# Token sums on their own partitions: the five norms of a two-block transformer kernel

## The reference

```
def rms_norm(x, g):
    xf = x.astype(jnp.float32)
    y = xf * lax.rsqrt(jnp.mean(xf * xf, axis=-1, keepdims=True) + NORM_EPS)
    return (y * g.astype(jnp.float32)).astype(x.dtype)

def layer_norm(x, g, b):
    mu = jnp.mean(xf, axis=-1, keepdims=True)
    var = jnp.mean(jnp.square(xf - mu), axis=-1, keepdims=True)
    return ((xf - mu) * lax.rsqrt(var + LN_EPS) * g + b).astype(x.dtype)

first block:   h = rms_norm(x, g_mix); mem_kv = rms_norm(mem, g_mem) @ w_mem_kv; attention, convolution, gates
               x = x + merged @ w_o;  h = rms_norm(x, g_ffn);  x = x + ffn(h);  x = rms_norm(x, g_final)
second block:  x = layer_norm(ALPHA * x + y @ w_out);  x = layer_norm(ALPHA * x + relu(x @ w_up)^2 @ w_down)
```

## Time and profile before

| | |
|---|---|
| median of 3 runs | 2922.84 us (2919.59 to 2927.17) |
| profiled execution, its own time | 2926.96 us |
| span of that profile | 2925.2 us, mean granted clock 0.982 |
| PE, PEld busy | 2784.8 us (95%), 2242.1 us (77%) |
| DVE, ACT, POOL busy | 1921.9 us (66%), 1017.2 us (35%), 1459.6 us (50%) |

### The profile page before, as it was taken

One profiled execution on the slowest core, in us unless ns is written; L12 is line 12 of the kernel. 1 busy time (PEld: TensorE's weight loads), 2 busy tenths in 40 slices (PEclk: granted clock), 3 DMA queues, 4 the chain that ended last, 5 costly groups with the idle time before them and its releaser, 6 DMA issues.

```text
span 2925.2 us, 35308 instructions
## 1 busy us (share of the span) xinstructions
PE 2784.8 (95%) x12634; PEld 2242.1 (77%) x12634; DVE 1921.9 (66%) x2515; ACT 1017.2 (35%) x1882; POOL 1459.6 (50%) x960
## 2 busy tenths in 40 slices
PE   7989999999999999999999889999898999999997
PEld 4777878886776877777777678888676888888885
DVE  3888999998536656655657558888747533444437
ACT  3352301117413333333333456666514211222223
POOL 2433344441242566666765326666642656666662
PEclk9999999999999999999999999999899999999999
DMA  4211122221231112112112300010111121111112
GB/s 150 54 44 37 37 72 80 83 81 51 95 114 37 44 47 61 52 44 58 44 51 67 113 15 30 23 30 23 73 43 36 37 58 43 57 57 50 50 44 72
DMA packets 44474, 165.04 MB, mean 56 GB/s; under 512 B 4969, under 2 KB 5609, under 8 KB 43313
## 3 DMA queue, kind: packets, MB, share of 16 engines
q1 hardware_dynamic: 38464, 132.00, 14.5%
q10 hardware_dynamic: 5872, 31.23, 2.8%
HBM read 145.61 MB, written 16.78 MB: 56 GB/s over the span
## 4 chain that ended last, share of the span: by engine, by line
PE 68%; DVE 10%; issue 6%; POOL 6%; POOLq 4%; ACT 4%; DMA 1%; DVEq 1%; ACTq 0%; SPq 0%
PE dense L800 9%; PE dense L801 9%; PE dense L804 9%; POOL w_lo L670 4%; PE dense L1265 3%; PE dense L1266 3%; PE dense L1268 3%; PE dense L1307 2%; PE side L1244 2%; PE dense L1308 2%; PE dense L1309 2%; PE side L1246 2%; PE side L1245 2%; PE side L1439 2%; PE side L1440 2%
## 5 line engine op out<-in xcount | busy, mean ns | idle before, releaser
L586 POOL TENSOR_TENSOR w_hi<-raw,zero 128x1024 fp32r<-128x1024 f32 x101 | 206.4, 2044 | 660.5 <-PE dense L804 464.7
L670 POOL TENSOR_TENSOR w_lo<-raw,w_hi 128x512 fp32r<-128x512 f32 x230 | 334.5, 1457 | 305.6 <-ACT w_hi L1858 177.4
L800 PE MATMUL dense<-a_hi,w_hi 128*128 128x512 f32 x944 | 373.6, 396 | 10.2 <-POOL w_lo L588 3.2
L801 PE MATMUL dense<-a_lo,w_hi 128*128 128x512 f32 x944 | 370.0, 392 | 0.0
L804 PE MATMUL dense<-a_hi,w_lo 128*128 128x512 f32 x944 | 292.4, 391 | 0.0
L588 POOL TENSOR_TENSOR w_lo<-raw,w_hi 128x1024 fp32r<-128x1024 f32 x101 | 270.5, 2678 | 7.9
L800 PEld LDWEIGHTS dense<-a_hi,w_hi 128*128 128x128 f32 x944 | 178.6, 189 | 52.1 <-issue 6.2
L804 PEld LDWEIGHTS dense<-a_hi,w_lo 128*128 128x128 f32 x944 | 178.5, 189 | 37.8
L801 PEld LDWEIGHTS dense<-a_lo,w_hi 128*128 128x128 f32 x944 | 178.7, 189 | 35.6
L644 POOL TENSOR_TENSOR stick_weights<-stick_weights,stay 128x511 f32<-128x511 f32 (+2 forms) x144 | 133.9, 932 | 112.2 <-DVE stay L2844 112.2
L800 PE MATMUL dense<-b_hi,w_hi 128*128 128x512 f32 x480 | 187.6, 391 | 0.2
(11 more groups left out here) (384 smaller groups left out, 7338.4 us busy)
## 6 DMA issues: line engine op xcount, KB each, us to landing
raw<-in_w_stream SPq DMA_DIRECT2D x229, 512.0 KB, 3.6
x_in<-in_x_t SPq DMA_DIRECT2D x8, 512.0 KB, 7.4
spill_gate<-T ACTq DMA_DIRECT2D x8, 512.0 KB, 2.6
spill_part<-gates ACTq DMA_DIRECT2D x8, 512.0 KB, 2.6
back<-spill_gate ACTq DMA_DIRECT2D x8, 512.0 KB, 3.8
back<-spill_part ACTq DMA_DIRECT2D x8, 512.0 KB, 4.7
x_res<-in_x_t ACTq DMA_DIRECT2D x2, 2048.0 KB, 9.1
spill_x<-x_res ACTq DMA_DIRECT2D x1, 4096.0 KB, 14.4
```

Of the source, the lines that this page charges most:

```text
L586: pool.tensor_tensor(w_hi[:, r % 2, :], raw[:, r, :], zero[:, 0:1].broadcast_to([P, D]), ALU.add).then_inc(weights_rounded, 1)
L670: return pool.tensor_tensor(w_lo[:, s, half], src, w_hi[:, s, half].bitcast(F32), ALU.subtract)
L800: pe.matmul(o, w_hi[:, slot, w], hi[:, k, x], start=b == 0, stop=False)
L801: pe.matmul(o, w_hi[:, slot, w], lo[:, k, x], start=False, stop=False)
```

## The change

The square and residual terms become the stationary operand and one column of a constant matrix, now holding 1/1024, the moving one: `own_part` issues four one-column products for 512 tokens, and the mean of each token comes out on its own partition, in four columns of `side[:, 0]`. The DVE step `own_sums` goes; ACT's root reads the four PSUM columns itself in norms 0 to 2 and for the memory. Norms 3 and 4 get `own_variance`, four small DVE operations. The mean is still spread over all partitions by 512-column products (`mean_part`), and the means are summed a second time as one-column products. `diagonal` goes; `spread_columns` multiplies the identity by a column of inverse roots read as a 128x128 broadcast, four products of 128 columns. In norm 0, DVE adds the first half's squares in pairs, so that four terms are left in place of eight.

```diff
-MATRICES = {"ident": 104, "ones": 104.5, "causal_q": 107, "strict_q": 107.5}
+MATRICES = {"ident": 104, "mean": 104.5, "causal_q": 107, "strict_q": 107.5}
...
-            def sum_part(src, c, at, start, stop):
-
-                return pe.matmul(side[:, at, c], ones[:, :], src[:, c], start=start, stop=stop)
+            def mean_part(src, h, start, stop):
+
+                return pe.matmul(side[:, 1, cols(h)], mean[:, :], src[:, cols(h)], start=start, stop=stop)
+
+            def own_part(to, src, start, stop):
+
+                for n in range(to.shape[-1]):
+                    last = pe.matmul(to[:, n:n + 1], src[:, P * n:P * n + P], mean[:, 0:1], start=start and n == 0, stop=stop,
+                                     skip_group_check=True)
+                return last
+
+            def spread_columns(to, values):
+
+                for n in range(values.shape[-1]):
+                    last = pe.matmul(to[:, P * n:P * n + P], values[:, n:n + 1].broadcast_to([P, P]), ident[:, :], start=True,
+                                     stop=True, skip_group_check=True)
+                return last
...
             def first_sums(h):
-                for k in range(KB):
-                    pe.wait_ge(x_squared, KB * h + k + 1)
-                    src = x_squares[:, k, :] if h else T[:, k // 2, cols(k % 2)]
-                    last = pe.matmul(side[:, 0, cols(h)], ones[:, :], src, start=k == 0, stop=k == KB - 1)
+                terms = KB if h else KB // 2
+                for k in range(terms):
+                    pe.wait_ge(x_squared, KB * h + k + 1) if h else pe.wait_ge(x_paired, k + 1)
+                    last = own_part(own_squares(h), x_squares[:, k, :] if h else T[:, k, cols(0)], k == 0, k == terms - 1)
                 last.then_inc(sum_ready, 1)
...
             def moments(norm, h, u):
 
                 pe.wait_ge(summed, summed_before(norm, KB - 3, h) + 1)
-                sum_part(T[:, 2, :], cols(h), 1, True, False)
+                mean_part(T[:, 2, :], h, True, False)
+                own_part(own_means(h), T[:, 2, cols(h)], True, False)
                 pe.wait_ge(added, added_before(norm, KB - 3, h) + 1)
-                sum_part(T[:, 3, :], cols(h), 0, True, False)
+                own_part(own_squares(h), T[:, 3, cols(h)], False, False)
                 out_evicted(pe, norm, u, KB - 2, h)
-                sum_part(x_res[:, KB - 2, :], cols(h), 1, False, False)
+                mean_part(x_res[:, KB - 2, :], h, False, False)
+                own_part(own_means(h), x_res[:, KB - 2, cols(h)], False, False)
                 pe.wait_ge(squares, squares_before(norm, KB - 2, h) + 1)
-                sum_part(T[:, (KB - 2) % 2, :], cols(h), 0, False, False)
+                own_part(own_squares(h), T[:, (KB - 2) % 2, cols(h)], False, False)
                 out_evicted(pe, norm, u, KB - 1, h)
-                sum_part(x_res[:, KB - 1, :], cols(h), 1, False, True).then_inc(mean_ready, 1)
+                own_part(own_means(h), x_res[:, KB - 1, cols(h)], False, True)
                 pe.wait_ge(squares, squares_before(norm, KB - 1, h) + 1)
-                sum_part(T[:, (KB - 1) % 2, :], cols(h), 0, False, True).then_inc(sum_ready, 1)
+                own_part(own_squares(h), T[:, (KB - 1) % 2, cols(h)], False, True).then_inc(sum_ready, 1)
+                mean_part(x_res[:, KB - 1, :], h, False, True).then_inc(mean_spread, 1)
...
-            def own_sums(norm, h):
+            def own_variance(norm, h):
...
+                dve.wait_ge(sum_ready, 2 * norm + h + 1)
+                dve.tensor_copy(own_mean[:, b], own_means(h))
+                dve.drain()
+                dve.tensor_tensor(own_square[:, b], own_means(h), own_mean[:, b], ALU.mult)
+                dve.drain()
+                dve.tensor_tensor(own_var[:, b], own_squares(h), own_square[:, b], ALU.subtract)
+                dve.drain()
+                dve.tensor_scalar(own_var[:, b], own_var[:, b], 0.0, None, ALU.max).then_inc(own_ready, 1)
...
             dve.wait_ge(consts_in, CONSTS)
-            own_sums(0, 0)
+            for k in range(KB // 2):
+                dve.wait_ge(x_squared, 2 * k + 2)
+                dve.tensor_tensor(T[:, k, cols(0)], T[:, k, cols(0)], T[:, k, cols(1)], ALU.add).then_inc(x_paired, 1)
             inverse_roots(0, 0)
             for k in range(KB):
                 scale_input(k, 0)
                 if k:
                     low_part(k - 1, 0, x_in[:, k - 1, :], "h")
-                if k == 5:
-                    own_sums(0, 1)
...
-            own_sums(3, 0)
+            own_variance(3, 0)
             centre(3, 0, 0)
             inverse_roots(3, 0)
```

More of the change, by code:

```diff
@@ L274, in build @@
         mats = {name: at(name, [P, P], F32, kib) for name, kib in MATRICES.items()}
-        ident, ones = mats["ident"], mats["ones"]
+        ident, mean = mats["ident"], mats["mean"]
         small = at("small", [P, SMALL_N], F32, 109.5)
@@ L927, in memory_squares @@
                     pe.wait_ge(mem_squared, k + 1)
-                    last = pe.matmul(side[:, 0, 0:MEM], ones[:, :], mem_squares[:, k, :], start=k == 0, stop=k == KB - 1)
+                    last = own_part(side[:, 0, 0:2], mem_squares[:, k, :], k == 0, k == KB - 1)
                 last.then_inc(mem_sum, 1)
             def memory_spread():
-                pe.wait_ge(mem_diag, 1)
-                pe.matmul(side[:, 1, 0:MEM], ones[:, :], T[:, 2, 0:MEM], start=True, stop=True).then_inc(mem_spread, 1)
+                pe.wait_ge(mem_rstd, 1)
+                spread_columns(side[:, 1, 0:MEM], rstd[:, 0:2]).then_inc(mem_spread, 1)
             pe.wait_ge(consts_in, CONSTS)
@@ L1519, in root @@
                 b, eps = slice(4 * h, 4 * h + 4), EPS_LN if norm >= 3 else EPS_RMS
[L1520 to L1529, removed]
+                if norm >= 3:
+                    act.wait_ge(own_ready, 2 * (norm - 3) + h + 1)
+                else:
+                    act.wait_ge(sum_ready, 2 * norm + h + 1)
+                act.activation(std[:, b], own_var[:, b] if norm >= 3 else own_squares(h), ACT.Sqrt, bias=eps).then_inc(std_ready, 1)
             def high(norm, k, h, src, which):
@@ L1600, in _ @@
                 if t == 1:
-                    act.wait_ge(mem_own, 1)
-                    act.activation(std[:, 0:2], own_sum[:, 0:2], ACT.Sqrt, bias=EPS_RMS, scale=1.0 / D).then_inc(mem_std, 1)
+                    act.wait_ge(mem_sum, 1)
+                    act.activation(std[:, 0:2], side[:, 0, 0:2], ACT.Sqrt, bias=EPS_RMS).then_inc(mem_std, 1)
                     for k in range(KB):
@@ L1802, in _ @@
             root(1, 0)
-            diagonal(1, 0)
             round_first(T_FF)
@@ L1944, in _ @@
             root(2, 1)
-            for h in range(2):
-                diagonal(2, h)
             act.preload_act_table_set("exp_and_others")
@@ L2066, in _ @@
             root(3, 0)
-            diagonal(3, 0)
             round_first(T_FF2)
@@ L2294, in _ @@
             dve.wait_ge(mem_sum, 1)
[L2295 to L2299, removed]
-            dve.wait_ge(mem_std, 1)
-            dve.reciprocal(rstd[:, 0:2], std[:, 0:2])
-            dve.drain()
-            for n in range(2):
-                last = dve.tensor_scalar(T[:, 2, P * n:P * n + P], ident[:, :], rstd[:, n:n + 1], None, ALU.mult)
-            last.then_inc(mem_diag, 1)
+            dve.wait_ge(mem_std, 1)
+            dve.reciprocal(rstd[:, 0:2], std[:, 0:2]).then_inc(mem_rstd, 1)
             dve.wait_ge(mem_spread, 1)
@@ L2604, in normed_low @@
                                   ).then_inc(parts["h2"][1], 1)
-            own_sums(1, 0)
             inverse_roots(1, 0)
@@ L2614, in _ @@
                     add_out(KB - 1, 1)
-            own_sums(1, 1)
             normed_low(KB - 1, 0)
@@ L2767, in _ @@
             for h in range(2):
-                own_sums(2, h)
-            for h in range(2):
                 inverse_roots(2, h)
@@ L2901, in _ @@
                     add_mixed(KB - 1, 1)
-            own_sums(3, 1)
+            own_variance(3, 1)
             low_part(KB - 1, 0, x_res[:, KB - 1, :], "x3")
@@ L3011, in _ @@
             add_down(KB // 2, 1)
-            own_sums(4, 0)
+            own_variance(4, 0)
             centre(4, 0, 0)
@@ L3028, in _ @@
                 if k == 3:
-                    own_sums(4, 1)
+                    own_variance(4, 1)
                 if k == 4:
@@ L3128, in constants @@
     r = np.arange(P)
-    c = {"ident": np.eye(P), "ones": np.ones((P, P))}
+    c = {"ident": np.eye(P), "mean": np.full((P, P), 1.0 / D)}
     c["causal_q"] = np.where(r[None, :] <= r[:, None], 0.0, NEG)
```

52 lines of the change are left out of this document (16 added, 36 removed).

## The result

The changed kernel takes 2955.67 us (median of 5 runs, 2949.41 to 2958.09) against 2921.46 for the kernel before on the same chip: 1.0113 times as long, 95% interval 1.0102 to 1.0123, **slower by 1.1%, 34 us**. I had forecast 2924.5, with 2946 as the upper end.

A forecast was written before the change was run, and what follows sets the result against it. PE, 68% of the last-ending chain, was taken as the bound; DVE or ACT savings count only where PE waits. Terms -4.5 + 0.1 + 0.2 - 2.6 + 4.4 + 4.1 = +1.7 on 2922.84 gave 2924.5; range 2915 to 2946.

The forecast's parts named there:

- the falling clock: Rival: PE's clock control takes one-column runs for idling, longer runs end low; 2961 in full (0.15), 2940 in part (0.18).
- the eight-column run of 1.8 us: Before the change, 16 eight-column passes from 79.96 to 81.74 left the clock at 1.00; cited against the falling clock.
- The rival's sizes: Falling clock: `first_sums(1)` 3.6 + 2.7, norm 2 2.7 + 2.7 (some 4 shows), four `moments` 4.0 + 2.7 mostly; about +36.
- The short pass at 0.111 us: All high-clock one-column passes on PE: 0.111 us each, read from an eight-column row, so 512 tokens cost 0.89 against 0.86.
- The rival of a cheaper pass: Short passes on the path cost 0.08 us each, the sum falls by 9.4 to 2915; chance 0.07.
- Norms 3 and 4, +8.5: `moments` grows 2.76 us a call, 6 long and 48 short passes for 12 long; norm 3 +4.4, norm 4 +4.1.
- Norm 0, -4.5: First half -2.6, first product near 23.3, held by POOL's `w_lo`; second half -1.9, PE's two waits before the spread go.
- Norm 2, -2.6: ACT's 2.46 us of diagonals go, rounding comes about 2.2 earlier, PE's 2.23 us wait for the low part vanishes.
- Norm 1, +0.2: 24 short passes for 6 long, twice, +0.08 each, and two spreads; removing the diagonals is covered by PE's tiles.
- -6.8: Forecast for norms 0 to 2 with the memory: norm 0 -4.5, memory +0.1, norm 1 +0.2, norm 2 -2.6.

The follow-up runs named there:

- The last kernel: Against the kernel with 64-column squares except norm 1, means summed once, broadcast spreads: POOL's tile 1 `w_lo` waits for the first `a_lo`; 2918.81 us, 0.9988 of before.

## Why the prediction was wrong

**The step that failed: the clock, taken as 1.00 through all one-column runs.** I used high-clock pass times for every sum and gave the falling clock 0.33, in full 0.15. It is the cause: 28.0 of the 34.2 us, by the kernel that differs in nothing but columns. What the runs showed in its place is a granted clock of 0.50 from inside `first_sums(1)` on, passes about 0.21 us apart instead of 0.111, and some 5 us of ordinary products at 0.50 behind. What I had held against it, the eight-column run of 1.8 us that left the clock at 1.00, showed only that a short run passes; the kernel with 8 columns in the long runs loses as much as the one with one. I had called one column in 128 "hardly any work", and should have given that more weight than a busy share.

**The rival's sizes.** Priced in full it gave 2961; measured 2955.7. `first_sums(1)`: priced 3.6 longer, measured 11.05 - 7.25 = 3.8; behind it products at the low clock from 41.28 to 46.54, 5.3 us (5.4). Norm 2's sums: 8.16 - 5.47 = 2.7 (2.7). `moments` is where I priced too much: about 26 for four calls and what follows, measured 13.0. The calls themselves are 1.2, 4.3, 1.8 and 1.7 us longer than with 64 columns (I had 4.0 for each, and 2.0 more for the second), since the clock is high in part of each. And the short runs that I left at nothing, memory and norm 1, aren't nothing. Against the kernel with 64 columns, product by product, one column loses 5.3 us behind the first product and up to 70 us, 1.2 at the memory, 1.6 in norm 1's first half and 4.6 in norm 2; my rival's terms were 6.3, 0, 0 and 4.

**The short pass at 0.111 us: right.** 64 passes of 64 columns in 7.25 us with their tail, 32 of one column at the memory in 3.63. The rival of a cheaper pass is out: 64 columns or one, the distance stays at the high clock. It lies near the 107 ns that the page "TensorE: Matmul & The Clock Gate" of the Trainium skill, section "LDWEIGHTS (loading the stationary operand)", makes of 128 columns (128 / 1.2), and far from the floor of about 25 ns between small products that its section "Back-to-back issue gap" has. At the low clock the passes here are about 0.21 us apart, twice that figure.

**Norms 3 and 4, +8.5: right as far as the medians tell**, 8.8 give or take 4, and by the mechanism named, the means summed twice. The traces place less in norm 3: with 64 columns the kernel loses 2.7 us there (forecast +4.4) and 3.9 in norm 4 (+4.1). Norm 3's second call was mis-sized. Before, part of it ran at the low clock and it took 7.0 us; with 64 columns it took 8.10, +1.1, where I had added 2.8 to the slow run.

**Norm 0, -4.5.** First half right in size, -2.6 (15.76 for 18.33 from the first square), and in its cause, POOL's `w_lo` beside VectorE's `a_lo`; what I had not seen is that the spread alone reaches it. The Trainium skill ("SBUF — State Buffer", "Who interferes with whom") says that a DVE instruction with two SBUF inputs contends with a GpSimd instruction that reads SBUF. The last kernel's trace agrees: `a_lo` takes 0.69 us alone and 2.49 beside POOL. Second half near the forecast once the clock holds: 43.6 was 36.0 from the first square, and the seven traces with own sums of 64 columns in norm 0 have 35.5 to 36.6; the spread alone has 37.4.

**Norm 2, -2.6.** PE's waits for `w_lo` fall from 2.7 us in all to 0.7 with the spread alone and with own products too, as forecast, and between the products at 1600 and 1700 us all eight traces without one- or eight-column products gain 2.2 to 2.9 us on before. In the changed kernel the sums' 2.9 us more (8.16 - 5.31) and the low clock behind them eat it.

**Norm 1, +0.2: wrong** by the traces, +1.4 to +3.0 in its second half even with 64 columns, and for the clock again; the medians leave the size open.

**Open.** Without the one-column loss, norms 0 to 2 gave -1.8 (-5.8 to 0) by the medians and not -6.8. By the traces the parts came out nearer to the forecast: in the three with own sums of 64 columns in norms 0 to 2, norm 0 to its second scale gained 4.0 to 4.9 us on before (forecast 4.5), norm 2 gained 2.2 to 2.9 (2.6) and norm 1 lost 1.4 to 3.0 (0.2). Where the rest went isn't shown. Stretches in which the kernels are the same differ by several us from trace to trace (between 82 and 800 us by -0.7 to +3.1 against before, between 1700 and 2140 by -4.5 to +0.2), and the profiled execution of before, on which the sum was built, took 2926.96, 7 above the median of 35 runs.

## What to carry to other kernels

A narrow product isn't free because its load hides it: in this kernel a run of 64 passes of one column (or eight) with full loads halved the clock for the rest of itself and for 4 to 5 us behind it, while PE read 100% busy. Where the pass time doesn't depend on the columns, try moving more than you need: 64 cost no time a pass here and gave back 28 us. Then look at the clock in the run itself, since a busy share doesn't show it. And before crediting an earlier operand, ask what else gates the same consumer: twice here (pairs and own sums at the first product, then the moved wait) the time went into one POOL operation, the low part of weight tile 1.

## What the runs showed of the hardware

- In norm 0's second sums, 64 passes, with PE and PEld at 2.00 of 2.00 us and the same loads, the granted clock stayed at 1.00 with 64 columns and went from 1.00 to 0.50 within the run with 8 or 1. Passes are 0.11 us apart at 1.00 (64 in 7.25 us), and at 0.50 about twice that (11 in 2.00 us).
- Runs of 64-column passes that began at 1.00 stayed there (norm 0's second half, norm 2). Where the clock was low or fell as they began, they took longer than the 512-column ones in the same place (4.91 to 5.22 us against 2.74 to 4.43 in norm 1's second sums), and in norm 0's first half all 7.06 us went by at 0.21 us a pass.
- A broadcast column as the stationary operand: 8 passes of 128 columns took 1.05 us at the high clock, where the diagonal's two of 512 took 1.02.
- Beside a POOL subtraction of 2.35 us, DVE's subtraction of two SBUF blocks ended 0.55 us after POOL's and took 1.50, 2.31 and 2.49 us in three kernels; alone it took 0.69.
